# Output projections of two attention blocks in products of 512 columns, with weights in pieces of half the rows

## The chip, the cores and the metric

The kernel runs on one core of one Trainium2 chip. The metric is the device time of one launch in microseconds (us). The engines are TensorE (PE in the profile; PEld is its weight load), VectorE (DVE), ScalarE (ACT), GpSimd (POOL) and SyncE (SP), which issues the DMAs of the weights.

## The reference

Two transformer blocks of two layers each, on 512 tokens of width 1024, all in fp32. What matters here is the last projection of each layer, `w_out`, of 1024 × 1024:

```python
# first block, every layer
merged = merged + merge_g[:, :, n] * (yb @ w_branch[n])     # over 4 branches
out = merged @ w_out
return _layer_norm(DEEPNORM_ALPHA * x + out, ln_g, ln_b)

# second block, every layer
mix = jnp.concatenate([o_a * jax.nn.silu(g_a), o_b * jax.nn.silu(g_b),
                       o_c * jax.nn.silu(g_c), o_d * jax.nn.silu(g_d)], axis=-1)
x = x + jnp.einsum('bsm,md->bsd', mix, w_out[l])
```

The second block normalises `x` by its mean square at the start of each layer. Its attention C (a neighbourhood attention of four heads) is the last of four.

## The kernel before, in words

**Products.** Each fp32 product is made of three: both operands are split into a high part (rounded to the type that TensorE takes fast, `wh`, `xh`, `yh`) and a low part (the rest, `wl`, `xl`, `yl`), and PE does low × high, high × low, high × high (L1477, L1478, L1479) into one PSUM bank. One such three is a product step here; it takes 128 rows of the sum (one `k`) for one tile of 128 tokens. In the trace's names of these products the first is what moves (the weights' columns) and the second what is loaded in the array (the activations).

**Weights.** They come in the pieces of the list `WEIGHTS` (L260 to L281: name, rows of 128, columns), in order, with two buffers for each part. SP loads piece j into `wr` (L2441) once piece j−2 is split. The split is a row of steps `cast`, one for each 512 elements of a partition (a chunk): ACT copies `wr` to `wh` (L1635), and waits for the last product of piece j−2; then DVE (even chunks, L1983) or POOL (odd chunks, L2376) subtracts to get `wl`. PE waits for the chunks that its next product reads.

**Order.** `plan` (L294) writes one list of steps by hand, and every engine runs its own steps of it in that order. `wnext(name)` (L348) first puts what casts of the piece that it returns are still due, and then makes those of the next piece due. `tick` (L339) puts one due cast; inside a `gemm` a tick comes after every third `k` if another `k` follows (`pieces`, L363). While `st["hold"]` is set no cast is put. So casts of the next piece are laid between the products of the present one, and what is left stands ahead of its first product.

**Output projection, block 1.** `w_out` comes in pieces `wo` of 8 rows × 256 columns. Layer 0 has four (L936 to L959): for each piece the four tiles of tokens, in the first with `k` 0 to 5 of all tiles ahead of `k` 6 and 7; between the second and third piece stand the products of the memory's features for layer 1 (`mkv`). Layer 1 has eight (L908 to L935): four for tiles 0 and 1, then the same four again for tiles 2 and 3. The result of each product of 8 `k` goes to `resid` on DVE (L2148: x · alpha + product, on 256 columns; L2151: its statistics), and after the last one of a tile `bn_aggr` (L2157) and the norm follow. In layer 1 a sum of squares follows (`rms1`, on ACT, `rms2`), then the features of block 2.

**Output projection, block 2.** The rows 0 to 5 of the mix (attentions A, B and D) come in four pieces `wo2a` of 6 × 256 and run beside attention C as filler between its logits (L1499), its masks on DVE (L2198), its exponentials on ACT (L1616), its turns (L1538) and its values (`out_partial`, L1049). The partial sums are added to an accumulator on DVE (`acc`, L2318). Tiles 2 and 3 of the last piece come later (`out_left`, L1067). The last two rows (attention C) are `wo2b`, 2 × 1024, in products of 512 columns.

Of the kernel before, what the change touches and what calls it, by code (L numbers as in the profile page):

```python
# [10 lines left out]
ALU = mybir.AluOpType  # L11
# [248 lines left out]
def weights_in_order():  # L260

    out = []
    for l in range(2):
# [9 lines left out]
        out += [("wo", 8, 256, l, 256 * m) for _ in range(1 + l) for m in range(4)]  # L273
    for l in range(2):
# [4 lines left out]
        out += [("wo2a", 6, 256, l, 256 * m) for m in range(4)]  # L279
        out.append(("wo2b", 2, D, l, 0))  # L280
    return out  # L281


WEIGHTS = weights_in_order()


# [7 lines left out]
def plan(known):  # L294
# [536 lines left out]
    for l in range(2):  # L831
# [72 lines left out]
        def out_product(w, m, i):  # L904
            out_tile(m, i, drain(gemm("tok", w, 0, 256, ("m", l), range(8), tile=i)))

        late = []
        if l:  # L908
            two = [wnext("wo") for _ in range(2)]
            st["hold"] = True  # L910
            held = {(m, i): drain(gemm("tok", two[m], 0, 256, ("m", l), range(6), tile=i, end=False, stop=False))
                    for m in range(2) for i in range(2)}
            for m, i in held:
                out_tile(m, i, drain(gemm("tok", two[m], 0, 256, ("m", l), (6, 7), tile=i, b=held[m, i], start=False)))
                if i:
                    wdone(two[m])
                    st["hold"] = False
            for m in (2, 3):
                w = wnext("wo")
                for i in range(2):  # L920
                    out_product(w, m, i)
                wdone(w)
            late += [settle(i) for i in range(2)]
            for m in range(4):
                w = wnext("wo")
                for i in (2, 3):
                    out_product(w, m, i)
                    advance_late(late)
                    if m == 3:
                        run(features(2, i - 2))  # L930
                wdone(w)
# [4 lines left out]
        w = wnext("wo")  # L936
# [111 lines left out]

    def out_partial(l, before, box):  # L1049
        for m in range(4):  # L1050
            w = wnext("wo2a")
            held = {}
            if m == 0:
                for i in range(2):
                    held[i] = yield from gemm("tok", w, 0, 256, ("y2", l), range(4), tile=i, end=False, stop=False)
                rest_of(before)
            for i in range(2 if m == 3 else 4):
# [1510 lines left out]
```

How the kernel before makes its waits and increments, by code:

```python
    def wait_ge(self, sem, n):  # L134
        return self
# [16 lines left out]
    def wait_ge(self, signal, value):  # L152
        if self.seen.get(signal, 0) < value:
            self.seen[signal] = value
            self.e.wait_ge(signal.sem, value)
# [1213 lines left out]
        def weights_ready(j, upto):  # L1369
            c = (upto - 1) // 512
            w.wait_ge(w_lo, w_lo.at((j, c - c % 2)))
            if c:
                w.wait_ge(w_lo2, w_lo2.at((j, c - 1 + c % 2)))
# [1 line left out]
        def act_ready(act, k, upto):  # L1376
            what = act[0]
            if what == "x":
                w.wait_ge(a_lo, a_lo.at(("feat", act[1], upto, 1)))
            elif what == "mem":
                w.wait_ge(a_lo, a_lo.at(("feat", f"mem{act[1]}", 1, 1)))
            elif what == "nq":
                w.wait_ge(y_lo, y_lo.at(("normed", act[1], 2)))
            elif what == "nkv":
                w.wait_ge(y_lo, y_lo.at(("normed", act[1], 4)))
            elif what == "mr":
                w.wait_ge(a_lo, a_lo.at(("mergeup", act[1])))
            elif what == "y":
                w.wait_ge(y_lo, y_lo.at(("out", act[1], "fox" if act[2] == 2 else "sb", 1)))
            elif what == "m":
                w.wait_ge(a_lo, a_lo.at(("merged", act[1], k)))
            elif what == "y2":
                w.wait_ge(y_lo, y_lo.at(("out", act[1], "B", 1)))
                if k >= 4:
                    w.wait_ge(a_lo, a_lo.at(("dsplit", act[1], k - 4)))
            elif what == "yc":
                w.wait_ge(y_lo, y_lo.at(("out", act[1], "C", act[2])))
```

## Time and profile before

| | |
|---|---|
| median of 3 runs | 1513.04 us (1512.2 to 1513.24) |
| profiled execution | 1514.28 us, its span 1512.5 us |
| mean granted clock of TensorE | 0.983 |
| busy: PE, DVE, ACT, POOL | 1418.9, 854.7, 729.5, 384.2 us |
| instructions on PE | 8202 |

Busy time is what an engine spent in its instructions; the span is from the first to the last instruction. What lies beside PE costs nothing as long as PE does not wait for it.

### The profile page before, as it was taken

The page shows a single profiled execution, that of the slowest core. Times are in us where ns is not written, and L with a number is a line of the kernel's source. Part 1 is how long each engine was busy: PE and PEld are TensorE (multiplying, and loading weights), DVE is VectorE, ACT ScalarE, POOL GpSimd, SP SyncE. Part 2 cuts the span into 40 slices and gives each one's busy share as a digit, 9 for nine tenths or more (in the row PEclk, how much of TensorE's full clock was granted, in tenths as well). Part 3 has the DMA queues.
Part 4 walks back from the last instruction along what each step waited for, and adds up shares of the span by engine and source line. Part 5 has one row for each costly group of instructions (what it writes and reads, how often), then busy time and mean ns, then how long its engine had stood idle before and what let it go on. Part 6 is the DMA issues. An engine that isn't in the chain of part 4 may idle for free.

```text
span 1512.5 us, 21589 instructions
## 1 busy us (share of the span) xinstructions
PE 1418.9 (94%) x8202; PEld 1101.7 (73%) x8202; DVE 854.7 (57%) x1553; ACT 729.5 (48%) x1557; POOL 384.2 (25%) x273
## 2 busy tenths in 40 slices
PE   7999999999989999999988889997999989988997
PEld 6767677778987677787778856665778856665776
DVE  3655436456662653455577665457656474457655
ACT  3555446555244554555554544435444544445443
POOL 2232122345131322123553111311112112310111
PEclk9999999999999999999999999998999999998999
DMA  6413451126242221112265413511323422511311
GB/s 225 112 30 88 109 136 43 51 68 227 87 154 61 53 84 57 56 46 63 91 216 162 118 52 63 118 57 49 97 65 94 116 70 55 92 60 46 101 61 57
DMA packets 195373, 135.76 MB, mean 90 GB/s; under 512 B 91590, under 2 KB 185414, under 8 KB 195270
## 3 DMA queue, kind: packets, MB, share of 16 engines
q1 hardware_dynamic: 191494, 120.22, 29.0%
q10 hardware_dynamic: 3776, 14.16, 2.5%
q8 instruction: 66, 1.08, 0.3%
q14 instruction: 37, 0.30, 0.1%
HBM read 122.03 MB, written 12.32 MB: 89 GB/s over the span
## 4 chain that ended last, share of the span: by engine, by line
PE 74%; DVE 12%; ACT 7%; issue 3%; DMA 2%; POOL 1%; SPq 1%; ACTq 0%; DVEq 0%; POOLq 0%
PE pb L1477 19%; PE pb L1479 17%; PE pb L1478 17%; PE pb L1560 6%; PE pb L1499 6%; PE pb L1538 5%; ACT prob L1616 2%; ACT tmp L1616 2%; ACT wh L1635 1%; DVE wl L1983 1%; DVE xl L1990 1%; DMA wr<-w_out 1%; DVE prob L2235 1%; PE pb L1522 1%; PE pb L1510 1%
## 5 line engine op out<-in xcount | busy, mean ns | idle before, releaser
L2376 POOL TENSOR_TENSOR wl<-wr,wh 128x512 fp32r<-128x512 f32 x178 | 254.2, 1428 | 857.6 <-ACT wh L1635 853.6
L1477 PE MATMUL pb<-xh,wl 128*128 128x512 f32 (+1 forms) x880 | 356.1, 405 | 11.4 <-DVE xl L1990 8.5
L1479 PE MATMUL pb<-xh,wh 128*128 128x512 f32 (+1 forms) x880 | 327.7, 372 | 0.0
L1478 PE MATMUL pb<-xl,wh 128*128 128x512 f32 (+1 forms) x880 | 327.6, 372 | 0.0
L1983 DVE TENSOR_TENSOR wl<-wr,wh 128x512 fp32r<-128x512 f32 x208 | 169.5, 816 | 183.5 <-ACT wh L1635 183.2
L1635 ACT CAST wh<-wr 128x512 fp32r<-128x512 f32 (+1 forms) x386 | 218.9, 604 | 38.0 <-PE pb L1479 17.1
L1477 PEld LDWEIGHTS pb<-xh,wl 128*128 128x128 f32 x880 | 169.2, 192 | 82.3 <-issue 47.0
L1479 PEld LDWEIGHTS pb<-xh,wh 128*128 128x128 f32 x880 | 168.7, 192 | 29.9
L1478 PEld LDWEIGHTS pb<-xl,wh 128*128 128x128 f32 x880 | 169.6, 193 | 22.3 <-issue 3.6
L1477 PE MATMUL pb<-wh,xl 128*128 128x256 f32 x448 | 133.2, 297 | 16.5 <-DVE wl L1983 8.4
L1616 ACT ACTIVATE prob<-prob,small 128x512 f32<-128x512 f32 (+3 forms) x128 | 76.3, 597 | 138.6 <-DVE small L2198 138.5
L1538 PE MATMUL pb<-cst,prob 128*128 128x128 f32 x768 | 119.3, 278 | 12.7 <-ACT prob L1616 8.2
L1478 PE MATMUL pb<-wl,xh 128*128 128x256 f32 x448 | 128.8, 288 | 0.0
L1479 PE MATMUL pb<-wh,xh 128*128 128x256 f32 x448 | 128.7, 287 | 0.0
L1538 PEld LDWEIGHTS pb<-cst,prob 128*128 128x128 f32 x768 | 95.2, 143 | 41.9 <-issue 10.7
L1616 ACT ACTIVATE prob<-pb,small 128x512 f32<-128x512 f32 (+1 forms) x96 | 58.5, 612 | 117.5 <-DVE small L2185 64.8
L1616 ACT ACTIVATE tmp<-pb,cst 128x512 f32<-128x512 f32 (+3 forms) x128 | 82.5, 645 | 61.2 <-PE pb L1505 19.5
L1477 PEld LDWEIGHTS pb<-wh,xl 128*128 128x128 f32 x448 | 87.8, 196 | 23.3 <-issue 7.0
L2256 DVE COPY prob<-pb 128x512 f32<-128x512 f32 (+3 forms) x128 | 70.8, 553 | 42.6 <-PE pb L1538 41.8
L1868 ACT COPY prob<-pb 128x512 f32<-128x512 f32 (+3 forms) x128 | 61.4, 480 | 61.4 <-PE pb L1538 60.5
L1477 PE MATMUL pb<-wh,yl 128*128 128x256 f32 (+1 forms) x272 | 86.4, 318 | 3.0 <-DVE wl L1983 1.8
L1478 PEld LDWEIGHTS pb<-wl,xh 128*128 128x128 f32 x448 | 88.1, 197 | 0.7 <-issue 0.5
(197 smaller groups left out, 2443.1 us busy)
## 6 DMA issues: line engine op xcount, KB each, us to landing
wr<-w_in SPq DMA_DIRECT2D x39, 1024.0 KB, 5.2
wr<-w_out SPq DMA_DIRECT2D x14, 1024.0 KB, 5.4
wr<-w_in SPq DMA_DIRECT2D x48, 256.0 KB, 4.6
wr<-w_branch SPq DMA_DIRECT2D x48, 128.0 KB, 2.3
x<-prob SPq DMA_DIRECT2D x12, 512.0 KB, 3.3
wr<-w_out SPq DMA_DIRECT2D x48, 128.0 KB, 3.0
wr<-w_mem_kv SPq DMA_DIRECT2D x4, 1024.0 KB, 5.5
prob<-x ACTq DMA_DIRECT2D x2, 2048.0 KB, 10.6
```

The lines of the kernel that those rows point to most:

```text
L1477: e.matmul(ps, ll, rh, start=start, stop=False)
L1478: e.matmul(ps, lh, rl, start=False, stop=False)
L1479: t = e.matmul(ps, lh, rh, start=False, stop=stop)
L1499: t = e.matmul(bank(b)[:, 0:128 * (hi - lo)], lhs, rhs, start=True, stop=br not in ("mla", "sb"))
L1538: t = e.transpose(bank(b)[:, c], probs(p)[:, c], C("ident"))
L1560: t = e.matmul(bank(b)[64 * half:64 * half + 64, lo:hi], v_[:, j, vc:vc + 64], turns(s["t"][half])[:, j, lo - 256 * ih:hi - 256 * ih], sta ...
L1616: return e.activation(o, i, f, bias=C("zero", 0, i.shape[0]) if bias is None else bias, scale=scale, **kw)
L1635: e.copy(wh[:, j % 2, c0:c1], wr[:, j % 2, c0:c1]).then_inc(w_hi.sem, w_hi.mark((j, c)))
L1868: t = e.copy(turns(t_)[:, lo:hi, 128 * i:128 * i + 128], bank(b)[:, 0:128 * (hi - lo)].rearrange("p (j c) -> p j c", c=128))
L1983: t = e.tensor_tensor(wl[:, j % 2, c0:c1], wr[:, j % 2, c0:c1], wh[:, j % 2, c0:c1].bitcast(F32), ALU.subtract)
L2256: t = e.tensor_copy(turns(t_)[:, lo:hi, 128 * i:128 * i + 128], bank(b)[:, 0:128 * (hi - lo)].rearrange("p (j c) -> p j c", c=128))
L2376: t = e.tensor_tensor(wl[:, j % 2, c0:c1], wr[:, j % 2, c0:c1], wh[:, j % 2, c0:c1].bitcast(F32), ALU.subtract)
```

## The change

The pieces of both projections have half the rows and double the columns. In block 1, `woa` is rows 0 to 3 and `wob` rows 4 to 7, each of 512 columns; layer 0 has four pieces, layer 1 eight, as before. In block 2, `wo2l` is rows 0 to 2 and `wo2h` rows 3 to 5 of 512 columns, four pieces in a layer. Each product is of 512 columns, a full bank; a tile's bank is held from the first piece to the second. `resid` and `acc` work on 512 columns, and the statistics of a tile come from two parts instead of four. The order of pieces, tiles and casts is written anew. The load of the memory's features is also given two semaphores instead of one.

```diff
-        out += [("wo", 8, 256, l, 256 * m) for _ in range(1 + l) for m in range(4)]
+        out += [("wo" + rows, 4, 512, l, 512 * m) for m in range(2) for rows in "ab"] if not l else []
+        out += [("wo" + rows, 4, 512, l, 512 * m) for _ in range(2) for rows in "ab" for m in range(2)] if l else []
...
-        out += [("wo2a", 6, 256, l, 256 * m) for m in range(4)]
+        out += [("wo2" + rows, 3, 512, l, 512 * m) for m in range(2) for rows in "lh"]
...
+        def out_rows1(w, i, b=None):
+
+            return drain(gemm("tok", w, 0, 512, ("m", l), range(4, 8) if b else range(4), tile=i, b=b, start=not b,
+                              end=bool(b), stop=bool(b)))
+
+        def out_half(tiles, beside):
+
+            held = {}
+            for m in range(2):
+                w = wnext("woa")
+                for i in tiles:
+                    held[m, i] = out_rows1(w, i)
+                    beside(None, i)
+                wdone(w)
+            for m in range(2):
+                w = wnext("wob")
+                for i in tiles:
+                    out_tile(m, i, out_rows1(w, i, held[m, i]))
+                    beside(m, i)
+                wdone(w)
...
-            two = [wnext("wo") for _ in range(2)]
-            st["hold"] = True
-            held = {(m, i): drain(gemm("tok", two[m], 0, 256, ("m", l), range(6), tile=i, end=False, stop=False))
-                    for m in range(2) for i in range(2)}
...
+            out_half((0, 1), lambda m, i: None)
             late += [settle(i) for i in range(2)]
...
+            out_half((2, 3), chains)
             late += [settle(i) for i in (2, 3)]
...
-        w = wnext("wo")
-        held = [drain(gemm("tok", w, 0, 256, ("m", l), range(6), tile=i, end=False, stop=False)) for i in range(4)]
+        w = wnext("woa")
+        held = [out_rows1(w, i) for i in range(4)]
+        wdone(w)
+        w = wnext("wob")
         for i in range(4):
-            out_tile(0, i, drain(gemm("tok", w, 0, 256, ("m", l), (6, 7), tile=i, b=held[i], start=False)))
-        wdone(w)
-        w = wnext("wo")
-        for i in range(4):
-            out_product(w, 1, i)
+            out_tile(0, i, out_rows1(w, i, held[i]))
         wdone(w)
         mem_features(1)
-        pair = [wnext("wo") for _ in range(2)]
+        pair = [wnext("woa"), wnext("wob")]
...
     def out_partial(l, before, box):
-        for m in range(4):
-            w = wnext("wo2a")
-            held = {}
+        for m in range(2):
+            w, held = wnext("wo2l"), {}
+            for i in range(3):
+                if i == 2 and m == 0:
+                    rest_of(before)
+                held[i] = yield from out_rows(l, w, i)
+                yield
+            w2 = wnext("wo2h")
+            st["hold"] = True
+            yield from out_sum(l, w2, m, 0, held[0])
+            yield
+            held[3] = yield from out_rows(l, w, 3)
+            wdone(w)
+            st["hold"] = False
+            yield
+            for i in (1, 2, 3)[:3 - 2 * m]:
+                yield from out_sum(l, w2, m, i, held[i])
+                yield
...
-                x = xres[:, i, 256 * m:256 * m + 256]
-                t = e.scalar_tensor_tensor(x, x, float(ALPHA), bank(b)[:, 0:256], ALU.mult, ALU.add)
+                x = xres[:, i, 512 * m:512 * m + 512]
+                t = e.scalar_tensor_tensor(x, x, float(ALPHA), bank(b), ALU.mult, ALU.add)
...
-                x = xacc[:, i, 256 * m:256 * m + 256]
-                t = e.tensor_tensor(x, x, bank(b)[:, 0:256], ALU.add)
+                x = xacc[:, i, 512 * m:512 * m + 512]
+                t = e.tensor_tensor(x, x, bank(b), ALU.add)
```

Two places where the change moves instructions, both on ACT, which starts every split. The lines of the changed kernel are 28 higher here (L1635 is L1663, L1616 is L1644, L1868 is L1896).

Block 2, layer 0, at the start of the filler beside attention C: `CAST wh<-wr` is a weight chunk, `ACTIVATE prob,small` an exponential of attention C, `COPY prob<-pb` a turned block copied out. Before:

```order
L1635 CAST wh<-wr 128x512
L1937 CAST yh<-scr 128x512
L1921 DMA scr<-norm_g 128x1024
L1635 CAST wh<-wr 128x512
L1616 ACTIVATE prob,small<-prob,small 128x512 x2
L1635 CAST wh<-wr 128x512
L1616 ACTIVATE prob,small<-prob,small 128x512 x2
L1868 COPY prob<-pb 128x4x128
```

and in the changed kernel:

```order
L1965 CAST yh<-scr 128x512
L1949 DMA scr<-norm_g 128x1024
L1644 ACTIVATE prob,small<-prob,small 128x512 x4
L1663 CAST wh<-wr 128x512 x3
L1896 COPY prob<-pb 128x4x128
L1644 ACTIVATE prob,small<-prob,small 128x512 x2
L1896 COPY prob<-pb 128x4x128
```

All three casts of the first `wo2h` now stand together behind the four exponentials of query tiles 0 and 1; layer 1 has the same rows.

Block 1, layer 1, from the pieces' casts through the norms of tiles 0 and 1 and their features (`ACTIVATE prob,stats` is the sum of squares of `rms1`, `CAST xh<-pb` a turned feature). Before:

```order
L1616 ACTIVATE stats<-stats,cst 128x1 x4
L1635 CAST wh<-wr 128x512 x6
L1616 ACTIVATE prob,stats<-prob,cst 128x1024
L1616 ACTIVATE stats<-stats,cst 128x1 x2
L1616 ACTIVATE prob,stats<-prob,cst 128x1024
L1616 ACTIVATE stats<-stats,cst 128x1 x2
L1635 CAST wh<-wr 128x512 x6
L1646 CAST xh<-pb 128x4x128 x2
L1635 CAST wh<-wr 128x512 x2
L1646 CAST xh<-pb 128x4x128 x2
L1635 CAST wh<-wr 128x512 x4
```

and in the changed kernel:

```order
L1644 ACTIVATE stats<-stats,cst 128x1 x4
L1663 CAST wh<-wr 128x512 x5
L1644 ACTIVATE prob,stats<-prob,cst 128x1024
L1644 ACTIVATE stats<-stats,cst 128x1 x2
L1644 ACTIVATE prob,stats<-prob,cst 128x1024
L1644 ACTIVATE stats<-stats,cst 128x1 x2
L1663 CAST wh<-wr 128x512 x7
L1674 CAST xh<-pb 128x4x128 x2
L1663 CAST wh<-wr 128x512
L1674 CAST xh<-pb 128x4x128 x2
L1663 CAST wh<-wr 128x512 x6
```

One cast has moved behind the sums of squares, and of those that stood ahead of the last two features one has moved behind them.

## Rows read from the trace of the kernel before

**Rows 1.** The page, busy time and the chain that ended last.
```profile
PE 1418.9 (94%) x8202; PEld 1101.7 (73%) x8202; DVE 854.7 (57%) x1553; ACT 729.5 (48%) x1557; POOL 384.2 (25%) x273
...
PE 74%; DVE 12%; ACT 7%; issue 3%; DMA 2%; POOL 1%; SPq 1%; ACTq 0%; DVEq 0%; POOLq 0%
```

**Rows 2.** Stretches: us; busy PE, PEld, DVE, ACT, POOL; clock, DMA share, GB/s.
```profile
364.10:391.22 27.12, 25.08 (x193) 24.41 (x192) 16.77 (x28) 7.46 (x14) 10.22 (x7) 0.94 0.37 120
392.88:416.56 23.68, 23.62 (x195) 23.17 (x193) 16.19 (x32) 5.57 (x12) 3.24 (x2) 1.00 0.19 67
...
770.44:788.61 18.17, 14.21 (x98) 12.98 (x96) 13.36 (x22) 8.44 (x17) 9.23 (x7) 0.91 0.35 117
788.61:811.90 23.29, 23.29 (x192) 23.10 (x192) 17.07 (x24) 9.81 (x19) 13.01 (x9) 1.00 0.54 170
811.90:834.55 22.65, 16.19 (x106) 15.65 (x105) 18.29 (x34) 9.08 (x18) 5.72 (x5) 0.85 0.64 151
1097.19:1154.22 57.03, 56.51 (x423) 45.39 (x421) 31.12 (x70) 25.39 (x57) 7.12 (x6) 1.00 0.23 61
1431.51:1488.54 57.03, 56.51 (x423) 45.38 (x421) 31.13 (x70) 25.39 (x57) 7.11 (x6) 1.00 0.13 42
```

**Rows 3.** Timeline of PE: start, us, engine, line, operation, out<-in (moving, loaded).
```profile
350.50 0.39 PE L1477 MATMUL pb<-yh,wl 128*128 128x512 f32 x1
...
363.87 0.39 PE L1479 MATMUL pb<-yh,wh 128*128 128x512 f32 x1
...
372.15 0.28 PE L1477 MATMUL pb<-wh,xl 128*128 128x256 f32 x1
...
385.70 0.28 PE L1479 MATMUL pb<-wh,xh 128*128 128x256 f32 x1
```

**Rows 4.** DMA issues: KB each, median us from issue to landing.
```profile
wr<-w_out SPq DMA_DIRECT2D x14, 1024.0 KB, 5.4
```

**Rows 5.** Timeline of PE, first products of layer 0's projection, with idle before.
```profile
365.51 0.36 PE L1477 MATMUL pb<-wh,xl 128*128 128x256 f32 x1 [0.54 <-POOL wl L2376]
...
367.65 0.46 PE L1477 MATMUL pb<-wh,xl 128*128 128x256 f32 x1 [1.20 <-DVE xl L2141]
```

**Rows 6.** Timeline of ACT behind the last product of layer 0's projection.
```profile
417.40 3.20 ACT L1635 CAST wh<-wr 128x512 fp32r<-128x512 f32 x6
...
426.52 0.62 ACT L1616 ACTIVATE stats<-stats,cst 128x1 f32<-128x1 f32 x2 [2.64 <-DVE stats L2157]
```

**Rows 7.** Timeline of PE, two waits of layer 1's projection.
```profile
788.61 0.35 PE L1477 MATMUL pb<-wh,xl 128*128 128x256 f32 x1 [1.91 <-DVE wl L1983]
...
818.39 0.58 PE L1477 MATMUL pb<-wh,xl 128*128 128x256 f32 x1 [3.44 <-DVE wl L1983]
```

**Rows 8.** Timeline of DVE, layer 1's last two aggregates.
```profile
839.33 0.37 DVE L2157 BATCH_NORM_AGGREGATE stats<-stats 128x2 f32<-128x24 f32 x2
```

**Rows 9.** Timelines of PE, DVE, ACT and POOL in block 2, layer 0.
```profile
1101.12 0.39 PE L1477 MATMUL pb<-wh,yl 128*128 128x256 f32 x1 [0.52 <-DVE yl L2344]
...
1102.73 1.13 PE L1499 MATMUL pb<-setB 64*128 64x512 f32 x4
...
1155.77 0.47 PE L1477 MATMUL pb<-wh,yl 128*128 128x512 f32 x1 [0.70 <-DVE wl L1983]
...
1103.89 0.69 DVE L2198 CUSTOM_DVE_ANT_0 prob<-pb,setB 128x512 f32<-128x512 f32 x1 [0.99 <-PE pb L1499]
...
1106.69 0.69 DVE L1983 TENSOR_TENSOR wl<-wr,wh 128x512 fp32r<-128x512 f32 x1 [1.49 <-ACT wh L1635]
...
1106.06 0.60 ACT L1635 CAST wh<-wr 128x512 fp32r<-128x512 f32 x1
...
1102.24 1.27 POOL L2376 TENSOR_TENSOR wl<-wr,wh 128x512 fp32r<-128x512 f32 x1 [16.25 <-ACT wh L1635]
```

**Rows 10.** Short stretches behind two idle times of PE; columns as in rows 2.
```profile
786.00:790.00 4.00, 2.09 (x18) 1.92 (x17) 3.93 (x7) 3.62 (x7) 3.21 (x3) 1.00 0.02 5
818.40:822.00 3.60, 3.60 (x17) 3.60 (x18) 1.99 (x5) 3.35 (x8) 1.08 (x1) 0.53 1.03 258
```

More of the change, by code:

```diff
@@ L284 @@
 WEIGHTS = weights_in_order()
+FIRST_ROW = {"wob": 4, "wo2h": 3}
 LOGS, TANHS, GATES = "natural_log_exp_and_others", "exp_and_others", "sigmoid_and_others"
@@ L365, in pieces @@
             over = k + 1 >= len(ks)
-            put("mm", ks=ks[k:k + 1], k0=ks[0], first=at["start"] and k == 0, last=end and over, stop=stop and over,
+            put("mm", ks=ks[k:k + 1], k0=ks[0], row=FIRST_ROW.get(WEIGHTS[at["j"]][0], 0), first=at["start"] and k == 0, last=end and over, stop=stop and over,
                 done=False, **at)
@@ L902, in out_tile, with chains @@
             give(b)
-        def out_product(w, m, i):
-            out_tile(m, i, drain(gemm("tok", w, 0, 256, ("m", l), range(8), tile=i)))
+        def out_rows1(w, i, b=None):
[15 more added lines that the diff above has]
+                wdone(w)
         late = []
         if l:
-            two = [wnext("wo") for _ in range(2)]
-            st["hold"] = True
-            held = {(m, i): drain(gemm("tok", two[m], 0, 256, ("m", l), range(6), tile=i, end=False, stop=False))
-                    for m in range(2) for i in range(2)}
[L913 to L918, printed above, removed]
-                w = wnext("wo")
-                for i in range(2):
-                    out_product(w, m, i)
-                wdone(w)
-            late += [settle(i) for i in range(2)]
-            for m in range(4):
-                w = wnext("wo")
[L926 to L931, printed above, removed]
+            def chains(m, i):
+                advance_late(late)
+                if m == 1:
+                    run(features(2, i - 2))
+            out_half((0, 1), lambda m, i: None)
+            late += [settle(i) for i in range(2)]
+            out_half((2, 3), chains)
             late += [settle(i) for i in (2, 3)]
@@ L1047, in project, with out_rows, out_sum, out_left @@
         yield
-    def out_partial(l, before, box):
-        for m in range(4):
-            w = wnext("wo2a")
-            held = {}
-            if m == 0:
[L1054 to L1057, printed above, removed]
-                b = yield from gemm("tok", w, 0, 256, ("y2", l), range(4 if i in held else 0, 6), tile=i, b=held.get(i),
-                                    start=i not in held)
-                put("acc", l=l, m=m, i=i, b=b)
-                give(b)
-                yield
-            if m < 3:
-                wdone(w)
-        box["w"] = w
-    def out_left(l, w, i):
-        b = drain(gemm("tok", w, 0, 256, ("y2", l), range(6), tile=i))
-        put("acc", l=l, m=3, i=i, b=b)
-        give(b)
+    def out_rows(l, w, i, b=None):
+        return (yield from gemm("tok", w, 0, 512, ("y2", l), range(3, 6) if b else range(3), tile=i, b=b, start=not b,
+                                end=bool(b), stop=bool(b)))
+    def out_sum(l, w, m, i, b):
+        yield from out_rows(l, w, i, b)
+        put("acc", l=l, m=m, i=i, b=b)
+        give(b)
+    def out_partial(l, before, box):
+        for m in range(2):
[6 more added lines that the diff above has]
+            w2 = wnext("wo2h")
+            st["hold"] = True
+            yield from out_sum(l, w2, m, 0, held[0])
+            yield
+            held[3] = yield from out_rows(l, w, 3)
+            wdone(w)
+            st["hold"] = False
+            yield
+            for i in (1, 2, 3)[:3 - 2 * m]:
+                yield from out_sum(l, w2, m, i, held[i])
+                yield
+            if m == 0:
+                wdone(w2)
+        box["left"] = w2, held
+    def out_left(l, left, i):
+        w, held = left
+        drain(out_sum(l, w, 1, i, held[i]))
     for l in range(2):
@@ L1141, in plan @@
                 for n in (2, 3):
-                    out_left(l, box["w"], n)
+                    out_left(l, box["left"], n)
                     advance_late(late)
-                wdone(box["w"])
+                wdone(box["left"][0])
                 st["hold"] = False
```

59 lines of the change are left out of this document (32 added, 27 removed).

## The prediction

> **What bounds the kernel now.** I read the page first, then the stretches of the four output projections, then the timelines inside them. TensorE (PE) is busy for 94% of the span and holds 74% of the chain that ended last, while DVE and ACT hold 12% and 7% of it [rows 1]. So a product that gets cheaper is paid in full where PE never waits, and a wait that the change puts in front of PE is paid in full as well. The stretches say where that is so [rows 2]. In block 1 the projections begin badly: 27.12 us for the first 192 products of layer 0, 18.17 us for the first 96 of layer 1. In block 2, where the projection is filler beside attention C, PE is busy for 56.51 of 57.03 us, in both layers alike. What the reader should see: block 1 has idle time to be won, block 2 has none, and only something to lose.
>
> All sums are made against the profiled execution (1514.28 us, span 1512.5); the median of the runs is 1513.04, 1.24 lower, and I take that off at the end. About 0.2% (3 us) is what a measurement of this kernel can tell from no change.
>
> **Step 1, the pace of a product.** From 372.15 to 385.70 us PE starts 113 products of 256 columns one behind the other, 13.55/113 = 0.120 us each. Products of 512 columns of the same three forms go from 350.50 to 363.87 us in 59 steps, 0.2266 us each [rows 3]. Two of the first cost 0.2398, one of the second 0.2266: 13.2 ns saved for each pair. The change turns 1344 products into 672: 192 pairs in each layer of block 1 (2.5 us), 144 in each of block 2 (1.9 us), 8.9 us in all. The loads keep their number in block 1 and their bytes everywhere, and the rows they read get longer; a piece lands in 5.4 us [rows 4], and it is asked for two pieces ahead, so I cost that edit at nothing (the splits of the piece before hide it; without them it would cost up to those 5.4 us once). DVE's adds come in half the number at double the width; what DVE gains by it lies beside PE (DVE is busy for 16 of the 24 us from 392.88 [rows 2]) and counts as nothing.
>
> The Trainium skill (TensorE: Matmul & The Clock Gate, "Back-to-back issue gap") puts a product of N columns at N/2.4 ns and a gap of 2.5 ns, so a merged pair would save 2.5 ns and the 672 pairs 1.7 us. The trace does not agree: its 256-column product takes 120 ns where that rule gives 109, its 512-column one 226.6 where it gives 216. I take the trace.
>
> **Step 2, block 1, layer 0.** The first 192 products need 23.04 us at their pace and take 27.12, so 4.1 us are lost. The waits stand in the timeline [rows 5]: 0.54 us for POOL's split, 1.20 us for `xl`, the low part of the activations' row 4, and the half clock behind them (mean 0.94). The new order does rows 0 to 3 for all four token tiles first; that is 48 products, 10.9 us, before any product reads row 4. So the second wait goes. POOL's two splits are late by about 0.5 us each at the narrower piece: 1.0 us stays. The stage ends at 364.10 + 96 × 0.2266 + 1.0 = 386.9 instead of 391.22; with the same 1.66 us for the memory's features and the 96 products behind them, the last product ends near 411.0 instead of 416.56. Then comes a tail that PE does not set: the last tile's norm waits until 426.52 [rows 6], 9.96 us behind the last product, because six casts (3.20 us) stand ahead of it on ACT and their splits ahead of it on DVE. The change leaves all six on ACT, in another place (four before the norm of tile 2, two after), so I keep the tail but for 0.7 us. Net: 426.5 − (411.0 + 9.3) = **−6.2 us**.
>
> **Step 3, block 1, layer 1.** Here the pieces are split only just in time [rows 2, 7]: PE waits up to 788.61 for the second pair (1.91 us at the end), and 3.44 us up to 818.39. With pieces of half the rows the first wait shrinks, as PE needs four rows of each piece, not all eight: the first pair ends at 785.05 by my queue (3.5 us earlier, 1.3 of it pace). Later the new order is worse. The order fences show ACT with five casts ahead of the sums of squares (`rms1`) where there were six, so the last casts of a `wob` piece stand behind two whole-row passes; PE waits 2.9 + 0.6 us there by my queue and about 0.75 us behind the last `resid`, instead of the 3.44, a shorter wait before it, and the half clock of 818.4. The last product ends at 827.1 instead of 834.55: −7.4. The next block's casts come later too (six after the features instead of four), so the aggregates of tiles 2 and 3, at 839.33 before [rows 8], come at 834.4: net **−4.9 us**, give or take 3.
>
> **Step 4, block 2, twice.** The pieces `wo2l` and `wo2h` have three rows, and a cast is put into the order only after every third product step that has another behind it. With three steps there is none. So all three casts of a piece stand together, directly ahead of its first product, and ACT meets them behind the four exponentials of query tiles 0 and 1 (the block 2 fences). Before, they stood singly between those rows. Follow it by durations [rows 9]: a logits product starts at 1102.73, DVE's mask at 1103.89 (+1.16), ACT's pair of exponentials behind it, and ACT is free for the cast at 1106.06, **3.33 us** behind the logits. Then the cast (0.6) and DVE's split (ready at 1107.38): **+4.65 us**. PE has left the logits at +1.06. It can start `wo2h` at +4.65 at the earliest: **3.5 us** of idle PE, and 0.6 more for POOL's split of chunk 1 (1.27 us). The second `wo2l` has one product step (0.68 us) between the logits and itself: 2.8. The second `wo2h` stands behind a copy rather than exponentials: 2.0 + 0.5. `wo2b` waits 1.45 + 0.7. That is 11.6 us for each layer. Before, the waits in this place were one up to 1101.12 and one at `wo2b` up to 1155.77, 0.52 and 0.70 us in their rows [rows 9], with the slow first product behind each 0.8 and 0.9: 1.7. So +9.9 − 1.9 for the pace = **+8.0 us for each layer, +16.0**.
>
> Bounds: an idle stretch may cost as little as the 0.7 us that `wo2b` waits for a split now (four of them 2.8 for a layer, which gives −0.8), and as much as 3.5 each (four of them 14, which gives +10.4). I stay near the upper end since the queue order is fixed and no shorter way past the exponentials exists.
>
> **Step 5, the clock.** Behind the idle of 3.44 us the granted clock was 0.53 for 3.6 us, the lower of the two levels (1.2 of 2.4 GHz); behind the 1.91 us up to 788.61 it stayed at 1.00 [rows 7, 10]. So of the new gaps only the longest should bring it. At half pace 3.6 us do the work of 1.9, and part of that stretch then lies beside attention's own waits: 1.1 us for each layer, **+2.2**. Between 0 and 1.7 × 3 × 2 = 10 us is open here.
>
> Sum: −6.2 − 4.9 + 16.0 + 2.2 = +7.1 us. 1514.28 + 7.1 = 1521.4; less 1.24 gives **1520**.
>
> **The rivals.** *Block 2 hides its casts, and the kernel is faster.* Its mechanism: ACT gets through the exponentials before PE arrives at the first `wo2h` product, so that this product waits as `wo2b` does now, 0.7 us. Then block 2 gives −0.8 for each layer, and the sum is −6.2 − 4.9 − 1.6 = −12.7: 1500.3. It decides at waits of 9.1 us for a layer instead of 11.6 (then block 2 costs 5.5 each and block 1 pays for it). For it: DVE is busy for only 31 and ACT for 25 of the 57 us [rows 2]. Against it: the chain logits, mask, exponential, cast, split is one of dependence, not of load. Faster by over 3 us: chance 0.12.
>
> *The two blocks cancel.* Waits of 8 to 10.5 us for a layer, no lower clock: 1513, within 3 us of it. Chance 0.18.
>
> *More is lost.* The half clock follows each of the three gaps of a layer (+1.1 each, +4.4 in all), or layer 1 of block 1 gains nothing since the casts behind `rms1` delay every later piece (+4.9): 1524 to 1530. Chance 0.10.
>
> *The pace does not improve.* If a 512-column product took twice what a 256-column one takes less 2.5 ns, step 1 would give 1.7 instead of 8.9 us, and the time would be 1527. The row of 0.2266 us speaks against it, for it comes from the same three lines of the kernel. Chance 0.03; this is the page's rule named in step 1.
>
> *The forecast*, 1516 to 1526: 0.57. So faster 0.12, same 0.18, slower 0.70. The range leaves out some 0.1 at either end: 1509 to 1527.
>
> **What the profile after will show.** Step 1: `wh,xl` and `wh,yl` products of 128x512 at starts 0.227 us apart. Step 2: no wait for `xl` after the second product step of the projection, and the first `mkv` features 6 us earlier. Step 3: a wait for `wl` of about 3 us between the `wob` pieces. Step 4: in each layer of block 2, three idle stretches of PE that end with DVE's `wl` split, 3.5, 2.8 and 2.0 us long, each with ACT's row of three casts right behind an exponential or a copy. Step 5: a stretch at clock 0.5 behind the first of them. If PE waits less than 1 us before the first `wo2h` product, the forecast is wrong and the kernel is faster.

## The result, and the profile after

The changed kernel takes 1539.12 us (median of 4 runs, 1538.22 to 1541.53) beside 1513.14 us for the kernel before (4 runs, 1512.2 to 1515.33): a ratio of 1.0171, 95% interval 1.0158 to 1.0185. It is slower by 26 us. The forecast was slower by 7 us, with 1527 as the far end of its range: the side was right and the size was not.

The page of the changed kernel, in the same lines as [rows 1]:

```profile
PE 1428.3 (93%) x7530; PEld 1070.6 (70%) x7530; DVE 857.8 (56%) x1505; ACT 729.4 (47%) x1557; POOL 382.4 (25%) x273
...
PE 75%; DVE 12%; ACT 8%; issue 3%; DMA 1%; POOL 1%; SPq 1%; ACTq 0%; DVEq 0%; POOLq 0%
```

672 products fewer, and yet PE is busy for 9.4 us more than before, over a span that is 27.2 us longer (1539.7 us). Busy time of PE that grows while its work shrinks is the first sign that its clock was lower; the mean granted clock is 0.972 where it was 0.983.

The stretches of the changed kernel, as in [rows 2]. The first and last are block 2's filler beside attention C, from the first `wo2l` product to the start of the last one before `wo2b`; the three between lie behind the first layer's waits:

```profile
1091.52:1161.07 69.55, 61.37 (x295) 40.97 (x294) 30.60 (x61) 24.57 (x56) 6.15 (x5) 0.90 0.19 50
1103.70:1109.20 5.50, 5.46 (x16) 4.33 (x17) 2.46 (x3) 0.30 (x1) 1.20 (x1) 0.50 0.29 80
1133.60:1136.70 3.10, 3.10 (x14) 2.35 (x12) 1.74 (x2) 0.59 (x1) 0.59 (x1) 0.50 0.12 40
1150.70:1154.70 4.00, 3.94 (x15) 3.26 (x16) 1.51 (x3) 0.00 (x0) 0.00 (x1) 0.57 0.63 137
1444.89:1512.03 67.14, 58.67 (x296) 38.88 (x294) 30.22 (x61) 24.58 (x56) 6.16 (x5) 0.95 0.12 36
```

Before, the same stretch took 56.91 us at clock 1.00 in both layers (57.03 up to the first product of `wo2b`, as in [rows 2]). Now it takes 69.55 and 67.14, at 0.90 and 0.95. PE's timeline of layer 0 shows the waits, in order, and what ended them; a row with brackets is the first product behind a wait:

```profile
1099.05 1.13 PE L1527 MATMUL pb<-setB 64*128 64x512 f32 x4
1103.74 0.79 PE L1505 MATMUL pb<-wh,yl 128*128 128x512 f32 x1 [3.57 <-DVE wl L2011]
1104.34 0.63 PE L1506 MATMUL pb<-wl,yh 128*128 128x512 f32 x1
1104.76 0.63 PE L1507 MATMUL pb<-wh,yh 128*128 128x512 f32 x1
...
1132.82 0.47 PE L1505 MATMUL pb<-wh,yl 128*128 128x512 f32 x1 [2.77 <-DVE wl L2011]
...
1149.53 0.50 PE L1505 MATMUL pb<-wh,yl 128*128 128x512 f32 x1 [1.59 <-DVE wl L2011]
...
1150.76 0.79 PE L1505 MATMUL pb<-wh,yl 128*128 128x512 f32 x1 [0.26 <-POOL wl L2404]
...
1163.38 0.47 PE L1505 MATMUL pb<-wh,yl 128*128 128x512 f32 x1 [1.92 <-DVE wl L2011]
```

From the start of the product before to the start of the product behind, these four waits (up to 1103.74, 1132.82, 1149.53 and 1163.38) are 4.16, 3.16, 1.99 and 2.31 us, where the pace would have been 0.52 (behind the last of the logits products, which starts at 1099.58) or 0.23: idle time of 3.6, 2.9, 1.8 and 2.1 us. The forecast had 3.5, 2.8, 2.0 and 1.45. What it had too small is seen in the distance between the products at 1104.34 and 1104.76: 0.43 us instead of 0.23, the pace at half the clock.

ACT shows the cause of the first wait, in the order that the fences ahead of the prediction gave: the pair of exponentials of query tile 1, then three casts.

```profile
1100.94 0.72 ACT L1644 ACTIVATE prob<-prob,small 128x512 f32<-128x512 f32 x1 [1.12 <-DVE small L2226]
...
1101.66 0.70 ACT L1644 ACTIVATE prob<-prob,small 128x512 f32<-128x512 f32 x1
...
1102.36 1.64 ACT L1663 CAST wh<-wr 128x512 fp32r<-128x512 f32 x3
```

The cast begins at 1102.36, 3.31 us behind the logits at 1099.05; the forecast had 3.33 from [rows 9].

The whole difference, followed through the two profiled executions by the same points of the program:

| from the same point to the same point | before, us | after, us | difference |
|---|---|---|---|
| start to the first changed product (unchanged code) | 364.10 | 366.18 | +2.1 |
| block 1, layer 0: to the norm of tile 3 on ACT | 62.42 | 57.08 | −5.3 |
| to layer 1's projection (unchanged code) | 343.92 | 342.34 | −1.6 |
| block 1, layer 1: to the last two aggregates | 68.89 | 66.20 | −2.7 |
| to block 2's first projection (unchanged code) | 257.86 | 259.72 | +1.9 |
| block 2, layer 0: filler beside attention C | 56.91 | 69.55 | +12.6 |
| `wo2b` and layer 1 up to its projection | 277.41 | 283.82 | +6.4 |
| block 2, layer 1: filler beside attention C | 56.91 | 67.14 | +10.2 |
| to the end of the span | 24.08 | 27.67 | +3.6 |

(The two 56.91 are from 1097.19 to 1154.10 and from 1431.51 to 1488.42, the start of the last product ahead of `wo2b`.) The sum is +27.2. Block 1 gave about 8 us, block 2 took 33. The first row, 2.1 us ahead of any changed product, is not the change's: three of the twelve profiles of this study, whose programs are the same up to there but for the semaphores, show it (first changed product at 366.2 us), the others stand between 363.3 and 364.3. Those three have a granted clock of 0.94 from 20 to 50 us, the other nine 1.00; here the changed kernel, then `fill`, an experiment below with the same program up to there:

```profile
20.00:50.00 30.00, 25.93 (x162) 23.53 (x161) 15.84 (x24) 11.73 (x22) 4.73 (x3) 0.94 0.34 101
```

```profile
20.00:50.00 30.00, 25.92 (x174) 23.54 (x173) 17.49 (x27) 12.35 (x22) 5.78 (x4) 1.00 0.33 101
```

So with the same code and the same busy time of PE (25.9 us) the clock can fall in one execution and not in another.

### The profile page after: what moved, and what is told of

It is laid out like the page before. It is cut to its first block, busy times and chain, and to the rows that moved or that the text cites. A ratio compares the mean times of both kernels' runs of the same rounds, so it can differ in the third digit from the quotient of the medians.

```text
span 1539.7 us, 20179 instructions
## 1 busy us (share of the span) xinstructions
PE 1428.3 (93%) x7530; PEld 1070.6 (70%) x7530; DVE 857.8 (56%) x1505; ACT 729.4 (47%) x1557; POOL 382.4 (25%) x273
## 4 chain that ended last, share of the span: by engine, by line
PE 75%; DVE 12%; ACT 8%; issue 3%; DMA 1%; POOL 1%; SPq 1%; ACTq 0%; DVEq 0%; POOLq 0%
PE pb L1505 19%; PE pb L1507 17%; PE pb L1506 17%; PE pb L1588 6%; PE pb L1527 6%; PE pb L1566 4%; ACT prob L1644 3%; ACT tmp L1644 2%; ACT wh L1663 1%; DVE wl L2011 1%; DVE xl L2018 1%; PE pb L1550 1%; DVE prob L2263 1%; POOL wl L2404 1%; PE pb L1538 1%
## 5 line engine op out<-in xcount | busy, mean ns | idle before, releaser
L2011 DVE TENSOR_TENSOR wl<-wr,wh 128x512 fp32r<-128x512 f32 x208 | 176.5, 853 | 179.2 <-ACT wh L1663 178.9
L1663 ACT CAST wh<-wr 128x512 fp32r<-128x512 f32 (+1 forms) x386 | 217.9, 604 | 34.7 <-DMA wr<-w_in 13.2
L1644 ACT ACTIVATE prob<-prob,small 128x512 f32<-128x512 f32 (+3 forms) x128 | 76.2, 596 | 146.8 <-DVE small L2226 146.7
L1566 PE MATMUL pb<-cst,prob 128*128 128x128 f32 x768 | 119.6, 281 | 12.7 <-ACT prob L1644 8.1
L1505 PE MATMUL pb<-wh,xl 128*128 128x256 f32 (+1 forms) x320 | 109.2, 341 | 14.3 <-DVE wl L2011 10.0
L1644 ACT ACTIVATE prob<-pb,small 128x512 f32<-128x512 f32 (+1 forms) x96 | 58.4, 612 | 115.6 <-DVE small L2213 63.1
L1644 ACT ACTIVATE tmp<-pb,cst 128x512 f32<-128x512 f32 (+3 forms) x128 | 82.5, 644 | 60.5 <-PE pb L1533 17.9
L1507 PE MATMUL pb<-wh,xh 128*128 128x256 f32 (+1 forms) x320 | 105.1, 328 | 0.0
L1506 PE MATMUL pb<-wl,xh 128*128 128x256 f32 (+1 forms) x320 | 105.0, 328 | 0.0
L1896 ACT COPY prob<-pb 128x512 f32<-128x512 f32 (+3 forms) x128 | 61.4, 480 | 83.3 <-PE pb L1566 82.4
L1505 PE MATMUL pb<-wh,yl 128*128 128x512 f32 (+1 forms) x176 | 74.6, 424 | 22.4 <-DVE wl L2011 20.0
L2425 POOL TENSOR_TENSOR yl<-tmp,yh 128x512 fp32r<-128x512 f32 x28 | 36.9, 1317 | 180.6 <-ACT yh L1908 180.6
L1505 PEld LDWEIGHTS pb<-wh,xl 128*128 128x128 f32 x320 | 61.3, 192 | 27.9 <-DVE wl L2011 10.7
```

What stands on the lines that cost most here:

```text
L1505: e.matmul(ps, ll, rh, start=start, stop=False)
L1506: e.matmul(ps, lh, rl, start=False, stop=False)
L1507: t = e.matmul(ps, lh, rh, start=False, stop=stop)
L1566: t = e.transpose(bank(b)[:, c], probs(p)[:, c], C("ident"))
L1644: return e.activation(o, i, f, bias=C("zero", 0, i.shape[0]) if bias is None else bias, scale=scale, **kw)
L1663: e.copy(wh[:, j % 2, c0:c1], wr[:, j % 2, c0:c1]).then_inc(w_hi.sem, w_hi.mark((j, c)))
```

## The experiments

The theory now was: block 2's late casts cause all of the loss, by the waits themselves and by the lower clock behind them; and the clock, which the forecast had at 2.2 us, costs nearly half as much as the 26 us that the whole change loses. Rivals: that part of the loss is block 1's; that the wide products themselves hold attention C up; that the clock is a by-product and costs nothing of its own.

### One block at a time

Block 1 as in the change, block 2 as before (`b1_only`):

```diff
-        out += [("wo2" + rows, 3, 512, l, 512 * m) for m in range(2) for rows in "lh"]
+        out += [("wo2a", 6, 256, l, 256 * m) for m in range(4)]
...
-                x = xacc[:, i, 512 * m:512 * m + 512]
-                t = e.tensor_tensor(x, x, bank(b), ALU.add)
+                x = xacc[:, i, 256 * m:256 * m + 256]
+                t = e.tensor_tensor(x, x, bank(b)[:, 0:256], ALU.add)
```

with `out_partial` and `out_left` as before. Expected:

> Block 1 as in the change, block 2 as before. The traces of before and after show the changed kernel 5 to 7 us ahead when block 2's projection begins. Theory (the whole loss is in block 2): 1506 to 1509 us. Rival (part of the loss is block 1's, as its last products run at the lower clock): 1512 to 1516.

Measured: 1507.62 us beside 1516.8 for the kernel before in the same session, a ratio of 0.9953 (0.9936 to 0.9969). It ran again in a later session, for the comparison with another kernel:

> The same kernel as b1_only (block 1 as in the change, block 2 as before), to stand beside the next one on the same chip: 0.5% faster than before, as there.

1507.75 beside 1515.45, 0.9948 (0.9932 to 0.9965). So block 1's change alone is worth 7 to 8 us.

Block 2 as in the change, block 1 as before (`b2_only`: the pieces `wo`, their loops, `resid` and `bn_aggr` as before):

> Block 1 as before, block 2 as in the change. Theory (the loss is in block 2, some 16 us for each layer): 1543 to 1547 us. If the two blocks' effects do not simply add, it comes out nearer to 1530.

Measured: 1545.7 beside 1516.8, 1.0212 (1.0188 to 1.0236), 32 us by the ratio. 0.9953 × 1.0212 = 1.0164, within the interval of the whole change (1.0158 to 1.0185): the two effects add, and block 2's is the whole loss. The two semaphores for the memory's features are in both kernels, so an effect of theirs would be in the product twice; none shows, and no run has them alone.

### The place of the casts

In `b2_early` one cast follows the second row of each three-row product of block 2:

```diff
-                if k % 3 == 2:
+                if k % 3 == 2 or len(ks) == 3 and k == 1 and WEIGHTS[at["j"]][0] in ("wo2l", "wo2h"):
                     tick()
```

> The changed kernel with one cast put after the second row of each three-row product of block 2, so that the casts of the next piece lie between the products of this one. Theory (the late casts cause both the idle of TensorE and the lower clock behind it): the three idle stretches of a layer go, and the time is 1503 to 1510 us. Rival (it is the wide products themselves, which hold up attention C and hold more banks): it stays above 1525.

Measured: 1509.55 beside 1516.8, 0.9961 (0.9945 to 0.9977). In `b2_clump` they stay in a row of three, but two tiles earlier:

```diff
                 held[i] = yield from out_rows(l, w, i)
+                while i == 1 and due:
+                    tick()
                 yield
...
                 yield from out_sum(l, w2, m, i, held[i])
+                while i == 2 and due:
+                    tick()
                 yield
```

> The changed kernel with the three casts of the next piece in one row as in the change, but placed two tiles earlier, ahead of the exponentials instead of behind them. Theory (the place in ACT's queue costs, not that they come in a row): as b2_early, 0.3 to 0.5% under before, no idle of TensorE over 1.2 us ahead of the three pieces. Rival (three casts in a row hold up the exponentials and so the turns): idle appears before the turns instead, and the time is over before's.

Measured: 1511.22 beside 1515.45, 0.9973 (0.996 to 0.9986), a shade less than expected. The stretch beside attention C, first of `b2_early`, then of `b2_clump`, both of layer 0:

```profile
1086.31:1141.79 55.48, 54.70 (x296) 37.05 (x294) 28.93 (x62) 24.33 (x56) 6.12 (x5) 1.00 0.24 63
```

```profile
1086.17:1140.82 54.65, 54.65 (x295) 36.91 (x294) 30.22 (x61) 24.73 (x56) 6.27 (x5) 1.00 0.24 64
```

The wide products hold nothing up. With the casts ahead of the exponentials the stretch takes 54.65 us, 2.3 less than before's 56.91, PE never idles in it and its clock is 1.00; and a row of three is no worse than three single ones. In `b2_clump` ACT does the three casts from 1088.40 to 1090.07, and the first exponential then waits for DVE and not for a cast:

```profile
1088.40 1.67 ACT L1667 CAST wh<-wr 128x512 fp32r<-128x512 f32 x3 [1.14 <-DVE yl L2376]
1092.94 0.72 ACT L1648 ACTIVATE prob<-prob,small 128x512 f32<-128x512 f32 x1 [2.88 <-DVE small L2230]
```

But neither is faster than `b1_only`, which has none of block 2's change. The gain comes back at `wo2b`, whose four casts still stand in a row ahead of its first product. PE in `b2_clump`:

```profile
1143.11 0.47 PE L1509 MATMUL pb<-wh,yl 128*128 128x512 f32 x1 [1.89 <-DVE wl L2015]
...
1144.75 0.47 PE L1509 MATMUL pb<-wh,yl 128*128 128x512 f32 x1 [0.71 <-issue]
```

For the second wait the profile names no releaser. Before, PE waited 0.70 us here [rows 9]. From the projection's start to the next layer's first product it is 75.02 us before, 74.75 in `b2_early` and 75.22 in `b2_clump`: what the pace gives, the wait at `wo2b` takes. By the order of steps, six-row pieces left room for casts of `wo2b` between products, and the three-row order, which keeps the last `wo2l` and `wo2h` alive together, does not; no run has `wo2b`'s casts moved by themselves.

### The clock by itself

`fill` keeps the late casts and fills PE's idle time with products that nobody needs. They are added to the bank or overwritten, so this kernel's sums in the output projection of block 2 are not the reference's.

```diff
+FILL = {('wo2h', 0): 15, ('wo2l', 512): 12, ('wo2h', 512): 7}
...
+                if (name_ := WEIGHTS[j][0:5:4]) in FILL and tile == 0 and s["ks"][0] == s["k0"]:
+                    for _ in range(FILL[name_]):
+                        e.matmul(bank(b), yh[:, 0, 0:128], yh[:, 0, 0:512], start=s["first"], stop=s["first"])
                 weights_ready(j, (s["ks"][-1] - s["row"]) * WEIGHTS[j][2] + c1)
```

> The changed kernel with 15, 12 and 7 extra products (512 columns of the activations' high part) ahead of the first product of the first wo2h, the second wo2l and the second wo2h, in the time in which TensorE waits for their casts. These add sums that the reference does not have. Theory (the waits of 3.6, 2.9 and 1.8 us are there all the same, but TensorE's clock falls because it idles): clock 1.00 behind them, 5 to 6 us less for each layer, 1527 to 1530 us. Rival (the clock is no part of it; the loss is the waits and a longer chain): 1539 us or a little more.

Measured: 1529.49 beside 1516.8, 1.0098 (1.0063 to 1.0133), where the change has 1.0171. Doing 34 more products a layer makes the kernel some 11 us faster (by the two intervals 5 to 17). Its stretches beside attention C, and the one behind the first filled wait:

```profile
1092.58:1156.85 64.27, 63.65 (x329) 42.90 (x328) 30.44 (x61) 24.64 (x56) 6.21 (x5) 1.00 0.21 54
1101.16:1111.00 9.84, 9.48 (x47) 6.70 (x46) 5.99 (x12) 4.21 (x9) 1.29 (x1) 1.00 0.26 67
1440.82:1505.05 64.23, 63.62 (x330) 42.91 (x328) 30.17 (x61) 24.60 (x56) 6.17 (x5) 1.00 0.12 38
```

64.27 and 64.23 us at clock 1.00, against 69.55 and 67.14. So 5.3 and 2.9 us of the changed kernel's stretches are the clock, where 5 to 6 were expected in each, and the remaining 7.4 over before's 56.91 are the waits less the pace. The profiled execution is the slowest of the four (1535.78 us): its clock fell elsewhere, behind `wo2b` among others.

`b2_only` has the same block 2 as the change, so its profile shows the same stretches a second time:

```profile
1098.30:1165.49 67.19, 58.66 (x295) 38.94 (x294) 30.52 (x61) 24.57 (x56) 6.15 (x5) 0.95 0.20 52
1448.60:1516.52 67.92, 59.73 (x295) 39.72 (x294) 30.30 (x61) 24.62 (x56) 6.18 (x5) 0.92 0.12 35
```

With the same waits, the clock costs 2.9 and 3.7 us there: its price differs from one execution to the next.

`fill_all` also fills the two waits at `wo2b` (8 products ahead of each of its first two product steps, 16 in a layer, where the expectation says 8) and two waits in layer 1 of block 1 (15 and 10), with sums there that are not the reference's either:

```diff
-FILL = {('wo2h', 0): 15, ('wo2l', 512): 12, ('wo2h', 512): 7}
+FILL = {('wo2h', 0): 15, ('wo2l', 512): 12, ('wo2h', 512): 7, ('wo2b', 0): 8}
...
+                if WEIGHTS[j][0] == "wob" and WEIGHTS[j][3] and tile == 2 and s["ks"][0] == 6:
+                    for _ in range(15 if WEIGHTS[j][4] == 0 else 10):
+                        e.matmul(bank(b), xh[:, 4, 256:384], h_[:, 0, c0:c1], start=False, stop=False)
```

> As fill, with 8 more extra products ahead of the first wo2b product of a layer, and 15 and 10 in block 1, layer 1, in the two waits between the wob pieces. Theory (the clock falls only where TensorE idles): clock 1.00 there too, and another 3 to 6 us less than fill's 1.0% over before: 0.6 to 0.8% over. Rival (fill's gain was all there is to have of the clock): 1.0% as in fill.

Measured: 1528.23 beside 1515.45, 1.0087 (1.0065 to 1.0108). The two stretches named, the first behind `wo2b` and the second in block 1:

```profile
1146.30:1176.46 30.16, 29.88 (x150) 23.73 (x151) 19.80 (x29) 11.08 (x22) 7.10 (x5) 1.00 0.50 116
805.00:815.00 10.00, 9.74 (x42) 7.54 (x42) 6.49 (x12) 4.78 (x10) 4.21 (x3) 1.00 0.69 161
```

The clock is 1.00 there too, as the theory said. The medians fell by 0.1% only, where 3 to 6 us were expected, but their intervals are too wide to decide on 3 us. The profiles show a gain: from block 2's first projection product to the last one of `wo2b` it is 84.97 and 82.69 us for the two layers, 2.1 and 2.0 less than in `fill` (87.03 and 84.69), although the 16 products take some 0.9 us more than the waits they fill (from the last product ahead of `wo2b` to the next layer's first it is 21.4 us, and 20.6 in `b2_clump` at clock 1.00). Taken together, 1.0171 − 1.0087 = 0.84%, some 12.7 us, about half of the 26 us, is clock; by the intervals it may be 9 to 17.

### Which wait brings the lower clock

`fill_12` is `fill` without the third filling, `fill_23` without the first.

> As fill, but only the two longer waits of a layer are filled (15 and 12 products); the third, 1.8 us ahead of the second wo2h, stays idle. If 1.8 us of idle alone bring the lower clock, it falls behind this wait as in the changed kernel (6 to 9 products at 0.43 us) and the time is some 2 to 3 us over fill's; if the fall needs the two waits before it, the clock stays at 1.00 and the time is fill's, 1.0% over before.

> As fill, but the first wait of a layer, 3.6 us ahead of the first wo2h, stays idle, and the second and third are filled. The clock falls behind the first alone, for about 5.9 us in layer 0 of block 2, which costs 3 us; in all 4 to 6 us over fill's time for both layers. If the falls feed each other, one shows behind the filled waits too.

Measured: 1532.92 beside 1514.04 for `fill_12`, 1.0121 (1.0091 to 1.0152), and 1533.89, 1.0128 (1.0098 to 1.0157), for `fill_23`. Two runs of each cannot part 2 us, so the traces decide. `fill_12`, its two stretches and the 4 us behind the wait that stayed:

```profile
1090.43:1154.69 64.26, 62.06 (x322) 41.61 (x321) 30.43 (x61) 24.63 (x56) 6.20 (x5) 1.00 0.21 54
1145.20:1149.20 4.00, 3.74 (x23) 2.96 (x22) 2.77 (x4) 0.59 (x1) 0.60 (x1) 1.00 0.42 96
1438.46:1502.68 64.22, 62.04 (x323) 41.59 (x321) 30.17 (x61) 24.60 (x56) 6.17 (x5) 1.00 0.13 38
```

With the two longer waits filled, the third (1.99 us from start to start, as in the change) brings no lower clock in either layer: 64.26 and 64.22 us, `fill`'s own numbers. In layer 0 of the changed kernel the same wait was followed by 0.57. And `fill_23`, where only the first wait stays:

```profile
1090.01:1155.78 65.77, 61.62 (x315) 41.37 (x313) 30.52 (x61) 24.58 (x56) 6.16 (x5) 0.97 0.20 53
...
1436.90:1503.27 66.37, 62.54 (x315) 42.14 (x313) 30.24 (x61) 24.63 (x56) 6.20 (x5) 0.95 0.12 37
1449.10:1454.70 5.60, 5.58 (x17) 4.38 (x17) 2.58 (x3) 0.29 (x1) 1.19 (x1) 0.50 0.33 89
```

It costs 1.5 us in layer 0 and 2.1 in layer 1 over `fill`, less than the 3 us and the 4 to 6 in all that were expected, and no fall shows behind the filled waits. So one wait of 3.6 us costs 1.5 to 2.1 us of clock beside itself, one of 1.8 us alone costs none, and the three together cost 2.9 to 5.3. Nor does the third bring a fall each time that the others are idle: in the changed kernel it did in layer 0 (0.57) and did not in layer 1, where the stretch behind it reads

```profile
1502.00:1507.00 5.00, 4.72 (x26) 3.77 (x27) 3.40 (x4) 0.87 (x2) 1.19 (x1) 1.00 0.00 0
```

In `b2_only` it brought none in either layer (from 1156.60 to 1160.60 and from 1507.60 to 1511.60 the clock is 1.00), so it is one fall in four with the longer waits idle, and none in two with them filled. That is too few to say that the longer waits matter to the third. What decides it stays open.

### Block 1, layer 1: a theory that fell

The forecast blamed the casts behind `rms1` for the wait between the `wob` pieces. `b1_rms` is `b1_only` with

```diff
             def chains(m, i):
+                while i == 3 and due:
+                    tick()
                 advance_late(late)
```

> As b1_only, but in block 1, layer 1, the casts that are due are put ahead of the norm and the sums of squares of tiles 0 and 1 instead of behind them. Theory (TensorE's waits of 3.6 and 2.1 us between the wob pieces come from casts queued behind rms1, and each brings the lower clock): both waits shrink under 1 us. As DVE's norms end the stage all the same, only part of the 6 to 7 us shows: 2 to 4 us less than b1_again. Rival (the norms of the stage set its end and the waits lie beside them): no change against b1_again.

Measured: 1507.58 beside 1515.45, 0.9947 (0.9929 to 0.9966); `b1_again` on the same chip 0.9948. No difference, and PE shows why: the waits did not go.

```profile
804.18 0.50 PE L1492 MATMUL pb<-wh,xl 128*128 128x512 f32 x1 [0.74 <-DVE wl L1998]
...
808.59 0.50 PE L1492 MATMUL pb<-wh,xl 128*128 128x512 f32 x1 [2.74 <-DVE wl L1998]
...
819.18 0.50 PE L1492 MATMUL pb<-wh,xl 128*128 128x512 f32 x1 [3.23 <-DVE wl L1998]
```

In `b1_again` the first two were one wait of 3.28 us, and the last was 2.02. DVE has the other half of the split and its own row of work, the norms of tiles 0 and 1. ACT had the four casts done by 800.80, but DVE split the third chunk only behind both norms:

```profile
798.61 2.19 ACT L1650 CAST wh<-wr 128x512 fp32r<-128x512 f32 x4 [1.59 <-DMA wr<-w_out]
...
804.75 1.28 DVE L2180 SCALAR_TENSOR_TENSOR prob<-prob,stats,setA 128x1024 f32<-128x1024 f32 x1
...
806.65 1.28 DVE L2180 SCALAR_TENSOR_TENSOR prob<-prob,stats,setA 128x1024 f32<-128x1024 f32 x1
807.85 0.68 DVE L1998 TENSOR_TENSOR wl<-wr,wh 128x512 fp32r<-128x512 f32 x1
```

So ACT's place in the queue was not the only bound there; DVE's norms are a second one of nearly the same length.

## Why the prediction was right or wrong

**Step 1, the pace: right in size, not shown by itself.** The products of the changed kernel start 0.2266 us apart. In `b2_clump`, where nothing waits, the stretch is 2.3 us shorter than before. It holds 126 of the layer's 144 pairs, so the pace of the forecast gives 1.7 of that, and the 0.5 to 0.7 us that PE waited up to 1101.12 in the kernel before [rows 9] is the rest.

**Step 2, block 1, layer 0: right.** The second wait, for `xl`, is gone, and the stage to the norm of tile 3 is 5.3 us shorter (forecast 6.2). The forecast's sum is off in itself: its terms put the last product near 410.3, not 411.0, which would have made it −6.9. The 1.0 us kept for POOL's splits did not come either; PE does not wait in the first 96 products, but it waits 1.10 us for DVE's split at 394.07, which was not foreseen. The tail from the last product to the norm, which I had put at 9.3 us, is 9.7: the projection ends at 413.57, and ACT's norm row of tile 3 stands at 423.26.

```profile
417.07 0.62 ACT L1644 ACTIVATE stats<-stats,cst 128x1 f32<-128x1 f32 x2 [3.78 <-DVE stats L2185]
...
423.26 0.62 ACT L1644 ACTIVATE stats<-stats,cst 128x1 f32<-128x1 f32 x2 [4.27 <-DVE stats L2185]
```

**Step 3, block 1, layer 1: the first waits right, the last one and the clock too small.** The first pair of pieces ends 4.2 us earlier than before (forecast 3.5; the pace gives 48 × 13.2 ns = 0.6 of it, not the 1.3 named there). The wait between the `wob` pieces was forecast at 2.9 + 0.6 us and is 3.27 + 0.24; the one behind the last `resid` was forecast at 0.75 and is 2.25, as DVE does its split (at 817.60) behind two norms (813.17 and 815.07) and the `resid`:

```profile
808.25 0.50 PE L1505 MATMUL pb<-wh,xl 128*128 128x512 f32 x1 [3.27 <-DVE wl L2011]
...
809.47 0.79 PE L1505 MATMUL pb<-wh,xl 128*128 128x512 f32 x1 [0.24 <-POOL wl L2404]
...
818.33 0.50 PE L1505 MATMUL pb<-wh,xl 128*128 128x512 f32 x1 [2.25 <-DVE wl L2011]
...
831.80 0.27 DVE L2185 BATCH_NORM_AGGREGATE stats<-stats 128x2 f32<-128x12 f32 x2
```

The last product started at 824.85 (59.3 us behind the layer's first; 64.0 before), and the aggregates came 2.7 us sooner by the stage's own length, where −4.9 was forecast. Up to the last product it is −4.8 where −7.4 was forecast. `b1_again` has 64.3 us for the stage to the aggregates, −4.6: the same instructions, with a mean clock of 0.97 up to the last product instead of 0.94, as one fall lies ahead of it instead of two. In block 1 as a whole −11.1 was forecast and 7 to 8 us measured.

**Step 4, block 2: right in mechanism, a fifth too small.** The three long waits beside attention C are those of the forecast to 0.2 us; at `wo2b` 2.1 + 0.9 us of idle came instead of 1.45 + 0.7. With the clock held up (`fill`) the two stretches are 7.4 us longer than before, and the wait at `wo2b` adds 2.5 in layer 0 (from the last product ahead of it to the next layer's first, 20.6 us in `b2_clump` and 18.1 before). That is some 20 us for two layers (2 × 7.4 and 2 × 2.5) against a forecast of 16.0.

**Step 5, the clock: the step that failed.** The forecast read its rows rightly: behind the idle of 3.44 us the granted clock was 0.53, and behind the 1.91 us up to 788.61 it stayed at 1.00. From these two it drew that "only the longest should bring it", and it took part of the slow time to lie beside attention's own waits, so that one fall in a layer costs 1.1 us. Both steps were wrong. In layer 0 of the changed kernel the clock fell behind every one of the waits, down to the 1.59 us of the third, and in layer 1 behind all but that one. And the slow time lay beside nothing: behind the first wait PE is busy for 5.46 of the 5.50 us at 0.50. The clock cost 5.3 and 2.9 us in the two stretches, 2.9 more behind layer 0's `wo2b` (from the last product ahead of it to the next layer's first it is 23.5 us in the changed kernel, 20.6 in `b2_clump` with the same wait and clock 1.00) and some 1.1 behind layer 1's (19.2 us from there to its last product, where the 15.6 of before and 2.5 for the wait would give 18.1): 12.2 us in the profiled execution, 9.3 in that of `b2_only`, counted in the same way. By the medians it is some 12.7 us for the whole kernel, block 1's two waits included. The forecast had 2.2. The rival that had the clock fall behind each of three gaps was named, within a chance of 0.10, but it too priced a fall at 1.1 us; the row from which it was priced [rows 10] shows 3.6 us at 0.53 of the clock, which is 1.7.

The sum, by the profiled executions: +27.2 us came and +7.1 was forecast. The clock in block 2 is 10.0 of the 20.1 us between them (12.2 for 2.2), the waits of step 4 are 3.6 (19.6 for 16.0), block 1 is 3.1 (−8.0 for −11.1). Of the other 3.4 us, 2.4 lie in the table's three stretches of unchanged code (2.1 in the first) and are no part of the change; 1.0 is not placed. The parts are read from one execution of each kernel, and the clock's share differs between executions by a few microseconds.

The rival *block 2 hides its casts* did not come, but `b2_early` is that case made on purpose, and its time, −0.4%, is not the 1500.3 that the rival gave: 3 to 4 us of the difference are block 1's smaller gain, and the rest is the pace gain of block 2, which `wo2b` takes back. The rule of the Trainium skill that the prediction names (TensorE: Matmul & The Clock Gate, "Back-to-back issue gap"), by which a merged pair saves 2.5 ns, is not borne out by the 0.2266 us either.

`b1_only` beats both kernels: 0.9953 and 0.9948 of the time before, in two measurements.

## What to carry to other kernels

Where an order written by hand lets work for the next piece ride between the products of this one, the length of the inner loop is part of that order: a loop cut from six or eight steps to three or four may no longer reach the point at which the rider gets on. Look then for who stands ahead of it on the slower engine. And price an idle stretch of TensorE at more than itself, since products behind it may run at the lower clock: here some 22 us of idle time in block 2 brought 9 to 12 us of clock on top. A kernel with extra products in the gaps tells the two apart. A gain in one stage counts only up to the next point at which the same queue is met, here `wo2b`.

## What the runs showed of the hardware

- Products that do nothing made the kernel faster: 34 of 512 columns a layer in idle time took the ratio from 1.0171 to 1.0098, and the granted clock of the two stretches from 0.90 and 0.95 to 1.00.
- The same wait of 1.99 us from start to start was followed by a clock of 0.57 in layer 0 of the changed kernel, and of 1.00 in its layer 1, in both layers of `b2_only` with the same waits ahead of it, and in both layers of `fill_12`, where the two longer waits ahead of it were filled. The length of one wait does not tell whether the clock falls.
- The same wait of 3.6 us was followed by 5.5 us at 0.50 in layer 0 of the changed kernel, and in `fill_23` by a shorter fall in layer 0 (4.8 us at a mean of 0.64, the row below) and 5.6 us at 0.50 in layer 1.
- From 20 to 50 us, in code that all twelve kernels share but for the semaphores, three profiles have a clock of 0.94 and nine 1.00, and the three reach the first changed product some 2 us later.

```profile
1102.20:1107.00 4.80, 4.44 (x14) 3.29 (x15) 1.95 (x2) 0.29 (x1) 1.19 (x1) 0.64 0.20 57
```
